# Two projection blocks taken together by halves of the contraction, and the later modulation tiles dealt out anew between TensorE and VectorE

## The reference, cut to what matters

```
mod = silu(c) @ w_ada + b_ada                   # [2048] x [2048 x 12288]
sh1, sc1, gt1, sh2, sc2, gt2 = split(mod, 6)
h = rmsnorm(x) * (1 + sc1) + sh1
proj = h @ w_in                                 # [256 x 2048] x [2048 x 3072]
xr, gr, xp = proj[:, :1024], proj[:, 1024:2048], proj[:, 2048:]
xr = causal_conv4(xr)                           # four taps along the tokens
hr = rg_lru(xr)                                 # gates, then a scan along the tokens
y  = [hr * gelu(gr), pool_mixer(xp)] @ w_out    # [256 x 2048] x [2048 x 2048]
x  = x + gt1 * y
```

## Time and profile before

| what | us |
|---|---|
| median of three runs | 2611.85 |
| the profiled execution's own time | 2609.51 |
| its span, first to last instruction | 2607.8 |
| TensorE busy in the span | 2561.5 |
| VectorE busy | 1580.7 |
| ScalarE busy | 1264.3 |
| mean granted TensorE clock, share of full speed | 0.995 |

### The profile page before, as it was taken

One profiled execution on the slowest core, in us unless ns is written; L12 is line 12 of the kernel. 1 busy time (PEld: TensorE's weight loads), 2 busy tenths in 40 slices (PEclk: granted clock), 3 DMA queues, 4 the chain that ended last, 5 costly groups with the idle time before them and its releaser, 6 DMA issues.

```text
span 2607.8 us, 32728 instructions
## 1 busy us (share of the span) xinstructions
PE 2561.5 (98%) x12532; PEld 2084.6 (80%) x12532; DVE 1580.7 (61%) x1894; ACT 1264.3 (48%) x1664; POOL 73.8 (3%) x156
## 2 busy tenths in 40 slices
PE   7899999999999999999999999999999999999999
PEld 1688878888888888888877788888888888888877
DVE  1449887764545455566787686456666666644435
ACT  3344444444444444454577555445555555544453
POOL 0012210100000000000000000000000000000000
PEclk9999999999999999999999999999999999999999
DMA  9999987875555555565544534555555555555554
GB/s 383 373 350 342 360 320 253 290 232 190 190 193 185 177 190 188 187 213 171 169 127 131 163 118 163 187 193 183 188 182 188 186 184 178 188 190 188 183 205 145
DMA packets 350157, 549.45 MB, mean 211 GB/s; under 512 B 18513, under 2 KB 200801, under 8 KB 349281
## 3 DMA queue, kind: packets, MB, share of 16 engines
q1 hardware_dynamic: 331616, 480.83, 55.5%
q0 software_dynamic: 18432, 67.12, 7.0%
HBM read 545.79 MB, written 2.10 MB: 210 GB/s over the span
## 4 chain that ended last, share of the span: by engine, by line
PE 90%; DMA 4%; DVE 3%; ACT 1%; issue 1%; SPq 0%; POOL 0%; DVEq 0%; ACTq 0%
PE pair L1311 27%; PE pair L1313 27%; PE pair L1312 27%; DMA mod_raw<-in_w_ada 3%; DVE w_lo L1959 1%; PE pair L1886 1%; PE pair L1286 1%; PE pair L1431 1%; PE pair L1287 1%; PE pair L1288 1%; DMA raw<-in_w_in 1%; DVE mod_acc L2180 1%; PE misc L1827 1%; PE misc L1939 1%; PE misc L1327 1%
## 5 line engine op out<-in xcount | busy, mean ns | idle before, releaser
L1959 DVE TENSOR_TENSOR w_lo<-raw,w_hi 128x1024 fp32r<-128x1024 f32 x848 | 1017.5, 1203 | 844.5 <-ACT w_hi L667 842.7
L667 ACT ACTIVATE w_hi<-raw 128x1024 fp32r<-128x1024 f32 x848 | 882.8, 1043 | 1039.4 <-PE pair L1313 959.6
L1311 PE MATMUL pair<-w_hi,a_hi 128*128 128x512 f32 x2048 | 810.4, 396 | 3.3 <-DVE a_lo L2068 2.5
L1313 PE MATMUL pair<-w_hi,a_lo 128*128 128x512 f32 x2048 | 799.3, 390 | 0.0
L1312 PE MATMUL pair<-w_lo,a_hi 128*128 128x512 f32 x2048 | 798.3, 390 | 0.0
L1311 PEld LDWEIGHTS pair<-w_hi,a_hi 128*128 128x128 f32 x2048 | 385.3, 188 | 84.3 <-issue 4.2
L1313 PEld LDWEIGHTS pair<-w_hi,a_lo 128*128 128x128 f32 x2048 | 385.1, 188 | 81.4
L1312 PEld LDWEIGHTS pair<-w_lo,a_hi 128*128 128x128 f32 x2048 | 385.6, 188 | 78.0 <-issue 1.0
L1311 PE MATMUL pair<-w_hi,hid_hi 128*128 128x512 f32 x704 | 275.0, 391 | 0.0
L1313 PE MATMUL pair<-w_hi,hid_lo 128*128 128x512 f32 x704 | 274.0, 389 | 0.0
L1312 PE MATMUL pair<-w_lo,hid_hi 128*128 128x512 f32 x704 | 273.9, 389 | 0.0
(11 more groups left out here) (368 smaller groups left out, 2157.8 us busy)
## 6 DMA issues: line engine op xcount, KB each, us to landing
raw<-in_w_in SPq DMA_DIRECT2D x88, 1024.0 KB, 5.3
raw<-in_w_up SPq DMA_DIRECT2D x176, 512.0 KB, 4.4
raw<-in_w_out SPq DMA_DIRECT2D x48, 1024.0 KB, 5.2
raw<-in_w_ffn_gate SPq DMA_DIRECT2D x88, 512.0 KB, 3.6
raw<-in_w_ffn_up SPq DMA_DIRECT2D x88, 512.0 KB, 4.6
mod_raw<-in_w_ada POOLq DMA_DIRECT2D x86, 512.0 KB, 6.8
raw<-in_w_ffn_down SPq DMA_DIRECT2D x32, 1024.0 KB, 5.1
raw<-in_w_down SPq DMA_DIRECT2D x32, 1024.0 KB, 5.1
```

The costliest lines, as they stand in the source:

```text
L667: run(w_hi[:, h % HALF_SLOTS, 0:n, :], raw[:, h // 2 % RAW_SLOTS, at0:at0 + n, :], ACT.Copy).then_inc(hi_ready, 1)
L1311: pe.matmul(o, hi[:, own], w_hi[:, slot, kk, :], start=(h == kk == 0), stop=False)
L1313: mm = pe.matmul(o, lo[:, own], w_hi[:, slot, kk, :], start=False, stop=(h == ph.halves - 1 and kk == n - 1))
L1959: dve.tensor_tensor(w_lo[:, slot, 0:n, :], raw[:, h // 2 % RAW_SLOTS, at0:at0 + n, :], w_hi[:, slot, 0:n, :].bitcast(F32), ALU.subtract).t ...
```

## The change

The halves p0 to p3 are now block 0 and p4 to p7 block 1, both over the first half of the contraction. p8 to p11 are block 0 and p12 to p15 block 1 over the second half. Six halves stand among the first modulation tiles instead of three, and four `w_in` tiles are loaded there instead of two. Units 1 and 3 accumulate in one bank of `misc`, as `pair` is taken. GpSimd may begin its ring as soon as the last first tile is used. Before, it waited for five halves. The taps of block 0 move to places 12 to 14, four instructions at each. The list of places and the order of the later tiles are new: 61 tiles instead of 64 stand beside `w_in`, and 35 instead of 32 beside `w_out`. In `order`, P is a tile for TensorE and D one for VectorE. The result of unit 6 now comes before that of unit 7.

```diff
-    mod_places = [0] * 6 + [2, 1] * ((IN_PLACES - 8) // 2) + [2, 2] + [2, 1, 1, 1, 1, 1, 1] * 4 + [0] * 4 + [1, 0] * (4 * up1.halves)
+    mod_places = [0] * 8 + [0, 3, 1, 3, 0, 2, 0, 3] + [1, 2, 1, 2, 1, 1, 1, 2] + [1, 3, 2, 2, 1, 1, 2, 2] + [3, 2, 2, 2, 0, 2, 1, 2] \
+        + [1, 3, 0, 2, 1, 1, 0, 2] + [1, 1, 1, 2] * 7 + [0] * 4 + [1, 0] * (4 * up1.halves)
...
-        order = "D" * 4 + "PPD" * 8 + "D" * 4 + "DDPP" * 8 + "D" * 32 + "D" * 32
+        order = "PPDDPPDPPPPD" + "DPPDPPDDDDD" + "DPPDPPDDDDPPDD" + "PPDPPPPPPPPDPP" + "DPPDDDDDDD" + "D" * 35 + "D" * 32
...
-    ROWS_AT, SUMS_AT, RESULT_AT = {28: 5, 52: 6}, {31: 5, 35: 4, 49: 7, 54: 6, 64: 8}, {34: 5, 39: 4, 54: 7, 59: 6}
-    MOD_SUMS = MOD_ORDER + [5, 4, 7, 6, 8, 9, 10, 11]
-
-    READ_BEFORE = {5: 4, 4: 5, 7: 6, 6: 6, 8: 7, 9: 7, 10: 9, 11: 9}
+    ROWS_AT, SUMS_AT, RESULT_AT = {30: 5, 45: 6}, {29: 5, 32: 4, 44: 6, 52: 7, 64: 8}, {33: 5, 36: 4, 48: 6, 56: 7}
+    MOD_SUMS = MOD_ORDER + [5, 4, 6, 7, 8, 9, 10, 11]
+
+    READ_BEFORE = {5: 4, 4: 5, 6: 4, 7: 6, 8: 8, 9: 8, 10: 9, 11: 9}
+
+    def in_half(p):
+
+        b, h = divmod(p, w_in.halves)
+        return (b, h) if b >= 2 else (h // 4, 4 * b + h % 4)
...
+        def first_bank(i):
+
+            return pair[:, 1, i, :] if i < 2 else misc[:, 2, :]
...
-        TURN0_AT, W_IN_AT = [(1, 9), (1, 13), (2, 1), (2, 4)], [(2, 15), (3, 5), (3, 11)]
+        TURN0_AT, W_IN_AT = [(1, 9), (1, 13), (2, 1), (2, 4)], [(2, 12), (2, 15), (3, 2), (3, 5), (3, 8), (3, 11)]
...
-                    pool.wait_ge(w_used, FIRST_SPLIT - 1)
+                    pool.wait_ge(mod_used, FIRST_TILES)
...
-            w_in_at = {2 * KC + 8: 0, 3 * KC: 1}
+            def load_in(b, j):
+                block, h = in_half(w_in.halves * b + 2 * j)
+                k0 = w_in.half_rows(h)[1]
+                load_tile(w_in, b, j, plain(d["w_in"][0], bass.ds(w_in_cols[block], COLS)), k0)
+
+            w_in_at = {2 * KC + 3: 0, 2 * KC + 9: 1, 2 * KC + 15: 2, 3 * KC + 5: 3}
...
+                    if (b, n) == (1, 4):
+
+                        act.wait_ge(w_used, w_in.half(1) + 4)
+                        conv_bias(0, 0, cw1[:, (CONV - 1) * RC:], cb1, xc, c1_bias)
...
-                if i >= 2 and k == 0:
-
-                    pe.wait_ge(mod_turned, i - 1)
-                mod_product(k, first_slot(s), pair[:, 1, i % 2, :])
+                if i == MOD_FIRST - 1 and k == 0:
+
+                    pe.wait_ge(mod_turned, i)
+                mod_product(k, first_slot(s), first_bank(i))
...
-                if b in (1, 2):
-                    conv_taps(n, (b - 1) % 2, 4 * (b - 1), cw1, CONV, RC, xc, c1_bias, c1_tap, 12 * (b - 1))
+                if b == 1 and 4 <= n < 7:
+                    for place in (2 * n - 8, 2 * n - 7):
+                        conv_taps(place, 0, 0, cw1, CONV, RC, xc, c1_bias, c1_tap, 0)
+                elif b == 2:
+                    conv_taps(n, 1, 4, cw1, CONV, RC, xc, c1_bias, c1_tap, 12)
```

More of the change, by code:

```diff
@@ L592, in _ @@
                 if s in w_in_at:
-                    load_tile(w_in, 0, w_in_at[s], plain(d["w_in"][0], bass.ds(w_in_cols[0], COLS)))
-            for j in range(len(w_in_at), w_in.tiles):
-                load_tile(w_in, 0, j, plain(d["w_in"][0], bass.ds(w_in_cols[0], COLS)))
+                    load_in(0, w_in_at[s])
             for b in range(1, w_in.blocks):
@@ L604, in _ @@
                     sp.dma_start(pool_w[:], d["w_pool"][0].rearrange("g (k p) n -> p (g k) n", p=P)).then_inc(mixw_landed, 16)
-                load(w_in, b, plain(d["w_in"][0], bass.ds(w_in_cols[b], COLS)))
+                for j in range(w_in.tiles):
+                    load_in(b, j)
             for b in range(w_out.blocks):
@@ L864, in _ @@
                     first_out(2)
-                    split_hi(w_in, 0, [2, 3])
+                    split_hi(w_in, 0, range(2, w_in.halves))
                     first_out(3)
-                elif q in (XG - 3, XG - 2):
-                    split_hi(w_in, 0, [q - 1])
+                elif q > XG // 2:
+                    split_hi(w_in, 1, [q - XG // 2 - 1])
             def mixer(b):
@@ L1284, in features_half @@
                         wh, wl = (w[:, slot, kk, m * P:(m + 1) * P] for w in (w_hi, w_lo))
-                        pe.matmul(o, wh, hi[:, k, :], start=(h == kk == 0 and m % 2 == 0), stop=False, skip_group_check=True)
+                        pe.matmul(o, wh, hi[:, k, :], start=(kh == kk == 0 and m % 2 == 0), stop=False, skip_group_check=True)
                         pe.matmul(o, wh, lo[:, k, :], start=False, stop=False, skip_group_check=True)
-                        mm = pe.matmul(o, wl, hi[:, k, :], start=False, stop=(h == ph.halves - 1 and kk == n - 1), skip_group_check=True)
+                        mm = pe.matmul(o, wl, hi[:, k, :], start=False, stop=(kh == ph.halves - 1 and kk == n - 1), skip_group_check=True)
                 mm.then_inc(w_used, 1)
[L1291 to L1296, removed]
             def tokens(ph, b, c, operand, beside=None, before=None):
@@ L1452, in mod_pair @@
                     pe.wait_ge(mod_turned, MOD_FIRST + MOD_BY_PE.index(a))
+                    pe.wait_ge(mod_ready, READ_BEFORE[a])
                 for j in (n - 1, n):
@@ L1471, in mods_beside, with half_in @@
                         mod_sums(a)
+            def half_in(p):
+                block, kh = in_half(p)
+                b, h = divmod(p, w_in.halves)
+                if b < 2:
+                    pe.wait_ge(n_lo, kh + 1)
+                features_half(w_in, b, block % 2, a_hi, a_lo, h, kh)
             def first_w_in(h):
-                pe.wait_ge(mod_ready, 2)
-                features_half(w_in, 0, 0, a_hi, a_lo, h, normed_yet(0))
+                pe.wait_ge(mod_turned, 2)
+                half_in(h)
             pe.wait_ge(c_ready, 1)
@@ L1490, in _ @@
             mod_turn(MOD_ORDER[MOD_FIRST - 1], MOD_FIRST)
-            first_w_in(3)
+            for h in range(len(W_IN_AT), w_in.halves):
+                first_w_in(h)
             def pools(h):
@@ L1506, in pools @@
                     mm.then_inc(pool_mm, 1)
[L1508 to L1512, removed]
+            pe.wait_ge(mod_ready, MOD_FIRST)
+            for b in range(1, w_in.blocks):
+                if 2 <= b < 4:
                     pe.wait_ge(c1_tap, 12 * (b - 1))
@@ L1515, in _ @@
                     pe.wait_ge(xp_ev, b - 3)
[L1516 to L1519, removed]
+                for h in range(w_in.halves):
+                    half_in(b * w_in.halves + h)
                     mods_beside(b * w_in.halves + h - LEAD)
@@ L2228, in _ @@
             norm_low(XG // 2 - 1)
-            split_lo(w_in, 0, [0, 1])
+            split_lo(w_in, 0, range(4))
             first_result(2)
-            split_lo(w_in, 0, [2, 3])
+            split_lo(w_in, 0, range(4, w_in.halves))
             first_result(MOD_FIRST - 1)
@@ L2333, in pooled_out @@
                                              op0=ALU.mult, op1=ALU.subtract).then_inc(pool_lo_ev, 1)
-            for b in range(w_in.blocks):
+            for b in range(1, w_in.blocks):
                 mixer(b)
```

32 lines of the change are left out of this document (12 added, 20 removed).

## The result

| | median us (runs) | ratio to before |
|---|---|---|
| before | 2609.77 (20) | 1 |
| after | 2614.65 (20) | 1.0018, 95% interval 1.0011 to 1.0025 |

The kernel became slower by 0.18%, some 4.9 us. 2610.5 had been forecast, 1.2 us faster than before. The profiled execution took 2617.10 us (span 2615.3), 2.5 above its own median; that of before lay within 0.3 of its own.

A forecast was written before the change was run, and what follows sets the result against it. TensorE was taken as the bound after 100 us, with full transfers before. Terms of -3.7 up to block 2, +0.9 for blocks 2 to 5 and +1.6 for the clock made -1.2: 2610.5 us, range 2600 to 2619.

The forecast's parts named there:

- part 1: Three more halves among the first tiles: 11.9 us gained, 5.2 us lost to two more `w_in` tiles moved there.
- the forecast for the transfers: First stage: 5.2 us more for two `w_in` tiles on a full stream, so the last first product ends at 105.2.
- the wait ahead of the sums: At place 32 TensorE waits 3.6 us for unit 5's result before summing unit 4, as VectorE does n39 first.
- the late tile of p16: Slower rival before block 2: p16's tile lands at 148, time 2620; chance 0.20 together with a full stream beside `w_out`.
- I take +0; up to +1 is possible: First stage: TensorE has just enough room, 28.6 us of work against 29.5 us of transfers, so no added time.
- That stays alike: 0: At p16: the clock's fall after idle time costs 1.6 us as before, so no change, 1.6 to either side.
- so +1.6 for the clock: After the 3.6 us wait at the sums of unit 4: the clock falls again and costs 1.6 us.
- With 5.5 us, between the two ends, n39 lands at 220.7: Ring tile n39, near place 32: landing 5.5 us after issue, between 3.8 and 6.8, makes a wait of 3.6 us.
- Part 4: Beside `w_out`: VectorE's three more products, 3.6 us over four blocks, cost 0; bound +3.9 us.
- the 2.9: Blocks 4 and 5: three of the earlier waits for `w_lo`, 2.9 us together, go as VectorE is relieved.
- part 2: New tile places up to block 2: n6 causes waits of 2.5 at p15 and 4.0 before block 2, net +3.2 us.
- the ring's rival: The ring keeps up, tiles n6 and n39 landing in 3.8 us: 2604, or 2597 without n6 holding VectorE; chance 0.30.

The follow-up runs named there:

- experiment 7: Experiment 3 with five halves among the first modulation tiles instead of six: 2602.38 us, ratio 0.9974.
- experiment 9: The kernel after the change, unchanged, timed and profiled a second time (the second profile): 2614.93 us, ratio 1.0019.
- experiment 2: The kernel after with another tile order in block 1, so VectorE needs no slot there that TensorE has just used: 2607.37 us, ratio 0.9990.
- experiment 8: The kernel after with ring tile n6 one place later, behind p15's split and four taps: 2611.54 us, ratio 1.0010.
- experiment 10: Experiment 6 with ring tile n39 one place later, behind p36's split: 2599.90 us, ratio 0.9963.
- experiment 12: Experiment 10 with ring tile n58 one place later, behind a split and three pooling operations: 2598.14 us, ratio 0.9953.
- experiment 6: Experiment 3 with one TensorE pair in block 3 a place earlier, so n39's slot comes free sooner: 2600.21 us, ratio 0.9966.
- experiment 3: The kernel after with experiment 2's order and the sums of unit 4 and their result three places later: 2603.07 us, ratio 0.9980.

## Why the forecast was wrong

**Right.** The mechanism of part 1; the forecast for the transfers (105.2, and 104.96 in experiment 7); n6's landing (6.8 forecast, 6.9 measured); the two waits that follow from it (2.5 and 4.0; measured 2.8 and 3.8); the wait ahead of the sums, through `READ_BEFORE`; no waits for `w_lo` in blocks 4 and 5, none at p31, none beside `w_out` but the one at its start. No `w_in` tile was late. Of the rivals, the late tile of p16 fell. The reading behind n6's landing is weaker than it looked, though: 3.8 us was taken as the price of an idle stream and 6.8 as that of a full one, but the stream ran at 253 GB/s (270.4 to 274.3) while the tile of 3.8 landed, and in experiment 9 a tile took 4.0 us at 377 (275.2 to 279.3). That a ring kept up would be worth much was right (experiment 2), though it needed another order and not quicker transfers.

**Wrong, by size.** The sum of -1.2 should have been about +5. Four steps failed:

1. *"I take +0; up to +1 is possible"* for TensorE's room in the first stage: it was +1.5 in the first profile (106.7). (The second ends at 107.8, but its first half also starts 1.3 later.) I had counted halves at 2.9 and every tile at the 0.54 of a long queue. In after a half between tiles takes 3.06 (101.75 to 104.81), and a tile on its own between two other kinds of work costs 1.05. Experiment 7 shows that TensorE and not the stream holds the end. Up to the end of p12 another 0.7 us is lost: p6 to p12 take 20.90 (108.39 to 129.29) instead of 20.34, 0.36 of it a wait. So p16 starts 2.4 late.
2. *"That stays alike: 0"* and *"so +1.6 for the clock"*. Before lost 1.5 us to the clock, at p16. In after p16 takes 5.4 us (2.4 lost), the sums and the next half lose 1.7 + 1.9, and the first halves of `w_out` take 18.2 instead of 16.6. That is 7.6 us, 6.1 more than before, where 1.6 more was forecast. The second profile has 7.3 that count (1.4 at p16, 4.3 from the sums to the pair behind the next half, 1.6 at `w_out`). This is the largest error, 4.5 us in the first profile.
3. *"With 5.5 us, between the two ends, n39 lands at 220.7"*: it took 6.6, and the wait was 5.0 instead of 3.6.
4. Part 4, *"I take 0"*, overlooked `pool_lo` at the start of `w_out`, where n58 needs the slot of n52. It cost 2.7 in one profile and nothing in the other. The rest of part 4 was right: apart from the clock, `w_out` shortens by 3.3 us, near the 3.1 that left it.

By the first profile the errors are 3.4 us up to the gates, 2.4 up to the pooling, 2.4 up to `w_out` and 1.3 behind it, less 0.9 in the rest: 8.6, and 2617.1 - 2608.3 = 8.8. By the medians the error is less, 4.9 + 1.2 = 6.1, as that execution was a long one. The forecast of 2610.5 is only 4.2 us from the 2614.65 measured, and that is luck: it was worked out from a median of three runs, 2611.85, and that of twenty is 2.1 lower. The stretch from gates to pooling is 0.8 us shorter than its own terms say (2.1 + 5.0 + 3.6 - 2.9 = 7.8 against 7.0). Most of this lies in the 2.9. Before, the three halves ahead of these waits last 4.54, 4.08 and 3.61 us from their start to that of the next half, 3.4 more than without a wait, where the rows show 2.95 idle. So a wait cost a little more there than its idle time. One pair of before also took 1.18 us instead of 0.99 (233.23 to 234.41).

The mechanism of the long waits did not fail. That the new halves gather the twelve taps behind p11 while the new list sets a tile that must wait for its slot just ahead of them stood in part 2, with its price of 2.5 + 4.0 us, and the waits came out at 2.8 + 3.8. The price of removing it stood under the ring's rival (6.5 + 1.6 = 8.1 us), and experiment 2 gave 8.8 up to the gates. What turned a forecast gain of 1.2 into a loss was the cost of the clock behind these waits, TensorE's room in the first stage, the wait for n39, longer than counted, and that for n58, not counted.

## What to carry to other kernels

Where two engines share a ring, an engine should not be made to use a tile whose slot the other has only just freed, while work that others wait for stands behind it in its queue. Put that work ahead of the tile: three such moves of one place (experiments 8, 10 and 12) gained 2.4, 1.9 and up to 2.7 us at their places, and freeing the slot 3.1 us earlier took 1.1 off the wait (experiment 6). Give TensorE's idle stretches a clock cost of their own (here 0 to 2.9 us for waits of 2 to 4.4 us, 3.3 to 4.3 for those of 5), and count single pieces of work between others at their single price, not at that of a queue.

## What the hardware showed that I had not expected

- The clock's fall doesn't follow the length of the wait alone. After 2.94 us of waiting at p36 the half took 3.05 us (experiment 3); at the same place after 2.77 it took 4.57 (experiment 7). After 1.18 at `w_out` the first six halves lost 1.6 (experiment 9), after 1.56 nothing (experiment 3) and after 3.77 they lost 2.9 (experiment 10). After the waits of 5.0 to 5.5 it fell in all five traces that have one (to 0.50 in 230 to 235 us of the kernel after) and cost 3.3 to 4.3.
- At the lower level the matmuls of a half start 0.21 us apart (147.56 and 147.77 in p16 of after), against 0.12 at full clock (103.05 and 103.17). The Trainium skill ("TensorE: Matmul & The Clock Gate", section "Part 1: The HAM clock gate (the "warmup" mystery)") gives two states of the clock, half and full, and calls its level binary. These spacings agree, as none lies between them but where the level changes, and a granted value such as 0.72 is then a mean over both levels: in 290 to 295 us the matmuls of `w_out` start 0.43 us apart up to 292.68 and 0.23 from 292.95 on, and 2.7 us at half with 2.3 at full make 0.73.
- A ring tile of 512 KB landed after 4.0 or 6.8 us at the same place of the same kernel. The stream moved 412 GB/s in the 2 us behind the issue of the early one and 365 behind that of the late one, so its rate there doesn't tell them apart; the cause stays open. Another tile landed after 9.2 us when it was issued sooner into a full stream (experiment 6), against 7.0 (experiment 3).
- A fall of the clock costs nothing while the work that it slows has a wait behind it: p15 took 1.4 us longer in experiment 9, and the wait for `xc` was 1.4 shorter.
